# Loading the scale ahead of the shift, and adding the shift to two products afterwards

## The reference

```python
mod = (jax.nn.silu(c) @ w_ada + b_ada).reshape(B, 6, D_MODEL)[:, :, None, :]
sh1, sc1, g1, sh2, sc2, g2 = [mod[:, i] for i in range(6)]
h = rmsnorm(x, norm1_g) * (1 + sc1) + sh1
proj = h @ w_in           # 1024 x 7696: q|k|v, beta, decay, z, pool input, gate_a, gate_b
```

## Time and profile before

| what | value |
|---|---|
| median of 3 runs | 1879.86 us |
| profiled execution | 1879.52 us |
| its span in the trace | 1877.5 us |
| TensorE busy | 1838.3 us, 98% of the span |
| VectorE / ScalarE / GpSimd busy | 82% / 46% / 41% |
| granted TensorE clock, whole span | 0.995 |
| HBM over the span | 252 GB/s |

### The profile page before, as it was taken

The page is one execution under the profiler, slowest core; times in us unless marked ns, Lnnn a source line. Parts: engine busy times, 40 slices in busy tenths (PEclk is TensorE's granted clock), DMA queues, the critical chain, the costliest instruction groups (busy, mean ns, idle before and its releaser), DMA issues.

```text
span 1877.5 us, 34737 instructions
## 1 busy us (share of the span) xinstructions
PE 1838.3 (98%) x13193; PEld 1669.2 (89%) x13193; DVE 1539.7 (82%) x3073; ACT 869.0 (46%) x1535; POOL 769.9 (41%) x572
## 2 busy tenths in 40 slices
PE   6999999999999999999999999999999999999998
PEld 3789999999878999999999888888888889888886
DVE  4667777777666889989794889899899899998998
ACT  3525544545342335688886434333333333333433
POOL 0000000000034435887782445555455555555662
PEclk8999999999999999999999999999999999999999
DMA  9732222222552326686778999999999999999984
GB/s 394 274 129 82 78 85 84 76 86 76 183 200 86 117 94 209 213 237 189 233 204 246 352 373 382 388 387 391 381 375 381 389 389 371 373 381 369 373 336 149
DMA packets 179732, 474.78 MB, mean 253 GB/s; under 512 B 16752, under 2 KB 79184, under 8 KB 176240
## 3 DMA queue, kind: packets, MB, share of 16 engines
q1 hardware_dynamic: 133488, 304.78, 46.5%
q0 software_dynamic: 46080, 167.79, 23.4%
HBM read 426.57 MB, written 45.94 MB: 252 GB/s over the span
## 4 chain that ended last, share of the span: by engine, by line
PE 54%; DVE 11%; DMA 2%; issue 1%; POOL 1%; ACT 0%; DVEq 0%; ACTq 0%
PE dd L2862 17%; PE pp L2849 16%; PE pp L2862 9%; PE pp L2466 7%; PE dd L2817 4%; DMA x<-in_v,idx 1%; POOL hot_a L2628 1%; DVE top_i L2509 1%; DVE top_i L2498 1%; DVE less L2499 1%; DVE top L3107 1%; DVE top_v L2504 1%; DVE top_v L2493 1%; PE pp L469 1%; DVE cand L3219 1%
## 5 line engine op out<-in xcount | busy, mean ns | idle before, releaser
L453 ACT ACTIVATE w_hi<-w_raw 128x1024 fp32r<-128x1024 f32 x202 | 212.8, 1054 | 146.1 <-PE pp L469 88.9
L457 DVE TENSOR_TENSOR w_lo<-w_raw,w_hi 128x1024 fp32r<-128x1024 f32 x176 | 216.2, 1229 | 31.2 <-ACT w_hi L453 31.0
L469 PE MATMUL pp<-act_hi,w_hi 128*128 128x272 f32 x1040 | 233.2, 306 | 1.0 <-POOL w_lo L2483 0.6
L469 PE MATMUL pp<-act_hi,w_lo 128*128 128x272 f32 x1040 | 214.8, 288 | 0.0
L469 PE MATMUL pp<-act_lo,w_hi 128*128 128x272 f32 x1040 | 214.5, 288 | 0.0
L3044 ACT ACTIVATE co_hi<-cf 128x384 fp32r<-128x384 f32 x126 | 66.3, 526 | 318.9 <-PE pp L2862 255.7
L2849 PE MATMUL pp<-act_hi,w_hi 128*128 128x384 f32 x616 | 208.8, 339 | 0.0
L2849 PE MATMUL pp<-act_lo,w_hi 128*128 128x384 f32 x616 | 207.6, 337 | 0.0
L2849 PE MATMUL pp<-act_hi,w_lo 128*128 128x384 f32 x616 | 207.1, 336 | 0.0
L2628 POOL TENSOR_SCALAR hot_a<-cst,gcols 128x128 f32<-128x128 f32 x144 | 190.2, 1329 | 40.4 <-PE dd L2817 40.0
L3337 DVE TENSOR_TENSOR v_lo<-v_raw,v_hi 128x1024 fp32r<-128x1024 f32 x126 | 154.0, 1222 | 28.8 <-ACT v_hi L3032 27.7
(11 more groups left out here) (501 smaller groups left out, 4584.3 us busy)
## 6 DMA issues: line engine op xcount, KB each, us to landing
w_raw<-in_stream SPq DMA_DIRECT2D x206, 512.0 KB
v_raw<-in_v SPq DMA_DIRECT2D x128, 512.0 KB
ada_w<-in_ada SPq DMA_DIRECT2D x24, 1024.0 KB, 10.6
gt<-gate_matrix SPq DMA_DIRECT2D x31, 768.0 KB, 9.2
gate_matrix<-gstage SPq DMA_DIRECT2D x11, 2048.0 KB, 10.3
early<-cst SPq DMA_DIRECT2D x50, 192.0 KB
cst<-early SPq DMA_DIRECT2D x50, 192.0 KB
wrow<-in_wout SPq DMA_DIRECT2D x8, 512.0 KB, 8.2
```

The source lines that it names most:

```text
L453: nc.scalar.activation(w_hi[k.slot][:], w_raw[k.slot][:], ACT.Copy).then_inc(w_hi_done, 1)
L457: nc.vector.tensor_tensor(w_lo[k.slot][:], w_raw[k.slot][:], w_hi[k.slot][:].bitcast(F32), ALU.subtract).then_inc(w_lo_done, 1)
L469: last = nc.tensor.matmul(pp[s][:, b, 0:HN], w[:, c * P:(c + 1) * P], a[:, c, b * HN:(b + 1) * HN], start=(c == 0 and w is w_hi[s] and a i ...
```

## The change

- The 8 MB for shift 1 and scale 1 are laid out anew: four pieces with the scale columns alone, each for two k, then four with the shift columns. The scale pieces are loaded first, chunk 0 ahead of them and chunk 1 behind them; then come the shift pieces.
- `modulate(k, half)` multiplies half a piece: 4 matmuls of 256 columns.
- The squares of x are summed over k by VectorE (7 additions, 128 x 544), so that the matmul with ones runs once instead of 8 times. ScalarE loads one table set for the logarithm and the exponential that follow.
- `h1` is made without the shift: x times scale times reciprocal root in one instruction for each k. Chunks 0 and 1 are multiplied with it. The shift modulates run between (before k = 7 of chunk 0).
- `shift_products(r)`: once the shift is there, 16 matmuls for each of chunks 0 and 1 multiply the weights, still in their buffers, with the 9 shift columns (20 and 10 columns wide with the low part and padding). The result is added when the pooling inputs are copied out (as the bias of `pool_evac`) and, for the samples, in `pool_group`.
- For chunk 2 onward `act_hi` and `act_lo` are made again with the shift in them: `shifted_hi(k)` on ScalarE and `shifted_low(k)` on VectorE, each once chunk 1 has used its k. GpSimd then adds the shift to `h1[k]` (8 instructions of 128 x 512), which only the beta and decay product reads.
- That product moves from behind chunk 1 to behind chunk 3, with pieces 9 and 10 behind it, then its folding and pieces 11 to 13. The cumulative sums of the decay move from in front of chunk 4 to behind it.
- SyncE's list: chunk 2 right behind the shift pieces; piece 8 waits for two shift modulates, with chunk 3, the beta and decay weights and all the rest behind it; pieces 11 to 13 stand behind chunk 4, 14 to 17 behind chunk 5.

```diff
@@ gpsimd
+                for k in range(KC):
+                    pool.wait_ge(h1_hi2, k + 1)
+                    pool.wait_ge(h1_lo2, k + 1)
+                    nc.gpsimd.tensor_scalar(h1[:, k, 0:TP], h1[:, k, 0:TP], mod[:, SH1 + k, 0:1], None,
+                                            ALU.add).then_inc(h1_whole, 1)
@@ sync
-                    if last is not None:
-                        sp.wait_ge(ada_used, last + 1)
+                    sp.wait_ge(ada_used, KC + last + 1 if last >= KC else KC + 2 * last + 2)
...
-                for i in range(KC):
-                    load_ada(i)
                 load_chunk(sp, Chunk(0))
+                for n in range(ADA_BUFS):
+                    sp.dma_start(ada_w[ADA_BUFS + n][:], ada_in[n]).then_inc(ada_ld[ADA_BUFS + n], 16)
                 load_chunk(sp, Chunk(1))
+                for n in range(ADA_BUFS):
+                    sp.dma_start(ada_w[n][:], ada_in[ADA_BUFS + n]).then_inc(ada_ld[n], 16)
+                load_chunk(sp, Chunk(2))
                 load_ada(8)
+                load_chunk(sp, Chunk(3))
...
                 load_chunk(sp, Chunk(4))
+                for i in range(11, 14):
+                    load_ada(i)
                 load_chunk(sp, Chunk(5))
+                for i in range(14, 16):
+                    load_ada(i)
@@ tensor
+                def modulate(k, half):
+
+                    pe.wait_ge(ada_ld[ADA_BUFS * (1 - half) + k // 2], 16)
+                    for j in range(4):
+                        last = nc.tensor.matmul(dd[32 * j:32 * j + NG, ADA_BANK[0], 256 * half:256 * (half + 1)], c_silu[:, k, :],
+                                                (scale_w, shift_w)[half][k][:, 256 * j:256 * (j + 1)],
+                                                start=(k == 0), stop=(k == KC - 1))
+                    last.then_inc(ada_used, 1)
...
+                    pe.wait_ge(shifts_ready, 1)
+                    to = dd[:, 2 + r, 256:256 + 2 * (NG + 1)]
+                    for c in range(KC):
+                        nc.tensor.matmul(to, w_hi[r][:, c * P:(c + 1) * P], shifts[:, c, :, :].rearrange("p s g -> p (s g)"),
+                                         start=(c == 0), stop=False)
+                        last = nc.tensor.matmul(to[:, 0:NG + 1], w_lo[r][:, c * P:(c + 1) * P], shifts[:, c, 0, :],
+                                                start=False, stop=(c == KC - 1))
+                    last.then_inc(pp_done[r], 1)
...
                 for c in range(KC):
-                    first_chunk(c)
-                    if c >= 5:
-                        ada(range(4 + c, 5 + c))
+                    scaled_chunk(0, c)
                     if c >= 3:
-                        second_chunk(c - 3)
+                        scaled_chunk(1, c - 3)
+                    if c == KC - 2:
+                        for k in range(KC):
+                            modulate(k, 1)
+                turn(1)
                 for c in range(KC - 3, KC):
-                    second_chunk(c)
-
+                    scaled_chunk(1, c)
+                for r in range(2):
+                    shift_products(r)
+                ada(range(8, 9))
+                for s in (own_hi, own_lo):
+                    pe.wait_ge(s, 1)
+                for c in range(KC):
+                    last = early_chunk(Chunk(2), c, h1_hi2, h1_lo2)
+                last.then_inc(pp_done[Chunk(2).slot], 1)
+
+                product(pe, Chunk(3))
                 pe.wait_ge(wba_ld, 32)
+                pe.wait_ge(h1_whole, KC)
+                pe.wait_ge(h1_own, 1)
...
-                product(pe, Chunk(2))
+                ada(range(9, 11))
                 pe.wait_ge(ba_out, 2)
...
-                ada(range(12, 14))
-                product(pe, Chunk(3))
+                ada(range(11, 14))
+                product(pe, Chunk(4), range(KC // 2))
                 ada(range(14, 16))
+                product(pe, Chunk(4), range(KC // 2, KC))
...
-                product(pe, Chunk(4), range(KC // 2))
-                turn(1)
-                product(pe, Chunk(4), range(KC // 2, KC))
+                turn(2)
                 ada(range(16, 17))
@@ vector
+                    nc.vector.scalar_tensor_tensor(out=h1[:, k, 0:TP], in0=x[:, k, 0:TP], scalar=aff1[:, k, 0:1],
+                                                   in1=rstd1[:, 0:TP], op0=ALU.mult, op1=ALU.mult).then_inc(h1_done, 1)
...
                 nc.vector.tensor_tensor(tmp_b[:], tok[:, ETOT], tok[:, GCUM], ALU.subtract).then_inc(gc_read, 1)
+                conditioning(2)
                 first_column(1, range(CW))
-                conditioning(1)
```

More of the change, by code:

```diff
@@ L662, in first_chunk, with scaled_chunk @@
                                                     stop=(c == KC - 1 and a is act_lo))
[L663 to L669, removed]
+                    if used is not None:
+                        last.then_inc(used, 1)
+                    return last
+                def scaled_chunk(r, c):
+                    early_chunk(Chunk(r), c, h1_hi_done, h1_lo_done, scaled_used if r else None)
@@ L670, in _ @@
+                for k in range(2):
+                    modulate(k, 0)
+                pe.wait_ge(sq1_summed, 1)
+                for b in range(2):
+                    last = nc.tensor.matmul(pp[0][:, b, 0:HN], ones, sq1[:, 0, b * HN:(b + 1) * HN], start=True, stop=True)
+                last.then_inc(ss1_done, 1)
+                for k in range(2, KC):
+                    modulate(k, 0)
                 turn(0)
-                ada(range(8, 9))
                 pe.wait_ge(rs1_done, 1)
                 for c in range(KC):
-                    first_chunk(c)
-                    if c >= 5:
-                        ada(range(4 + c, 5 + c))
+                    scaled_chunk(0, c)
@@ L733, in _ @@
                 product(pe, Chunk(C_HEADS), range(0, 1))
-                turn(2)
+                turn(3)
                 product(pe, Chunk(C_HEADS), range(1, 2))
@@ L821, in _ @@
                 first_evac(1)
-                ada_evac(1)
+                ada_evac(2)
                 first_square(1)
@@ L900, in _, with shifted_low, bias_summed @@
                 low(KC - 1)
+                def shifted_low(k):
+                    dve.wait_ge(h1_hi2, k + 1)
+                    nc.vector.scalar_tensor_tensor(out=act_lo[:, k, 0:TP], in0=h1[:, k, 0:TP], scalar=mod[:, SH1 + k, 0:1],
+                                                   in1=act_hi[:, k, 0:TP].bitcast(F32), op0=ALU.add,
+                                                   op1=ALU.subtract).then_inc(h1_lo2, 1)
+                def bias_summed(r):
+                    done(dve, Chunk(r))
+                    two = dd[:, 2 + r, 256:256 + 2 * (NG + 1)].rearrange("p (s g) -> p g s", s=2)
+                    nc.vector.tensor_reduce(first_bias[:, r, :], two[:, 0:NG, :], AX_X, ALU.add).then_inc(bias_read, 1)
+                conditioning(1)
+                shift = mod[:, SH1:SH1 + KC, :]
+                st(nc.vector.tensor_copy(shifts[:, :, 0, 0:NG], shift))
+                st.settle()
+                nc.vector.tensor_tensor(shifts[:, :, 1, 0:NG], shift, shifts[:, :, 0, 0:NG].bitcast(F32),
+                                        ALU.subtract).then_inc(shifts_ready, 1)
+                nc.vector.tensor_tensor(sample_cols(h1), sample_cols(h1), b, ALU.add).then_inc(h1_own, 1)
+                for k in range(2):
+                    shifted_low(k)
+                dve.wait_ge(own_hi, 1)
+                nc.vector.tensor_tensor(act_lo[:, :, TP:NT], own, act_hi[:, :, TP:NT].bitcast(F32),
+                                        ALU.subtract).then_inc(own_lo, 1)
+                bias_summed(0)
+                shifted_low(2)
+                split_lo(dve, Chunk(2))
+                shifted_low(3)
+                bias_summed(1)
+                for k in range(4, KC):
+                    shifted_low(k)
+                split_lo(dve, Chunk(3))
                 dve.wait_ge(pool_ld, 16)
@@ L1042, in _ @@
                     pool_read(n)
-                conditioning(2)
+                conditioning(3)
                 affine(aff2, SC2, "g2")
```

137 lines of the change are left out of this document (85 added, 52 removed).

## The result

The changed kernel takes 1887.74 us (median of 6 runs, 1884.99 to 1888.79), the kernel before 1880.85 us (6 runs beside it on the same chip, 1879.79 to 1882.84). The ratio is 1.0035, with an interval of 1.0025 to 1.0046: slower by 6.9 us. The profiled execution took 1887.96 us, its span is 1886.2.

What follows compares the result with a forecast made beforehand. TensorE's gapless list was taken to bound the first block. Start -11.4, list +8.0, gaps +1.0, clock +0.8, pieces +2.0 and decay sums +2.6 gave +3.0 on 1879.5: 1882.5 us, range 1876.5 to 1888 (8 in 10).

Steps and rivals of the forecast that it cites:

- rival 3: First block: more gaps than counted (later clock rise +1.6, third product's cover gone +1, slower shift_products +1.3); 1885 to 1887, chance 0.20.
- (c): Weight pieces 13 and 15 land late because their buffers come free later; TensorE waits 1.0 us for each, 2.0 together.
- the list: Work added to TensorE's list behind the start: shift modulates, piece 8, shift_products, two transposes, less saved switches; +8.0 us.
- rival 2: GpSimd's adds become the bound ahead of the beta and decay product; at 2.5 us each 1885.1 us, chance 0.10.
- rival 4: The early start doesn't come about, layout or queue holding the scale back (29 instead of 26.5); 1885.0 us, chance 0.05.
- Start: TensorE's first product begins at 26.5 instead of 37.98, as four pieces are awaited instead of eight; -11.4 us.
- the case for which I had 25.3: First product starts at 25.3 instead of 26.5 if the clock is full there.
- the term for grouping: Pieces and small work standing in groups save five TensorE switches at about 0.2 us each; -1.1 us.
- (a): At the first k, VectorE's slower h1 and chunk 1's split make TensorE wait near 30 us; 1.0 us.
- (b): Clock at the start: half until 31.7, 4.2 us at half instead of 3.3; +0.8 us (0 to 2.4).
- (d): Decay sums behind chunk 4 delay VectorE's chain; TensorE waits 2.6 us somewhere between norm_sums(1) and pool_out(1).
- The first: Rival: the gaps don't form, 4.6 us less, 1877.9 us; chance 0.22, half of that below 1876.1.

Runs made afterwards that it cites:

- run 3: Changed kernel with pieces 9 and 10 again before chunk 3 and the decay sums again between chunk 4's halves: 1880.91 us, 0.9999 of the kernel before.
- run 8: As run 3, with one of four column blocks in each shift modulate (16 matmuls instead of 64): 1881.13 us, one run.
- run 2: Changed kernel with pieces 9 and 10 multiplied in front of chunk 3 again: 1882.69 us, 1.0010 of the kernel before.
- run 4: Kernel before, with only the beta step, its fold, the decay sums and the pieces and steps belonging to them moved back: 1884.90 us, ratio 1.0024.
- run 11: Changed kernel with a second 128 x 512 GpSimd instruction (times one) behind each of the eight adds: 1899.70 us, one run.
- run 12: Changed kernel with GpSimd's adds on the first 128 of 512 columns only: 1889.54 us, one run.
- run 5: As run 3, with the shift modulates in pairs behind k = 1, 2, 4 and 5 of chunk 0: 1881.70 us, 1.0003 of the kernel before.
- run 6: As run 3, with two shift modulates ahead of the first product and piece 11 ahead of the fold: 1881.71 us, 1.0006 of the kernel before.
- run 10: As run 3, with each row of narrow shift matmuls run twice (64 instead of 32): 1886.98 us, one run.
- run 1: Changed kernel with the decay sums between chunk 4's halves again and first_column(1) ahead of conditioning(2): 1886.14 us, 1.0022 of the kernel before.

## Why the prediction was right or wrong

The direction held (3 us slower forecast, 6.9 measured), though the prediction gave 0.50 to no change that could be told and 0.38 to slower. 1887.74 lies in the range, close to its end; it is outside the likeliest case of 1880.5 to 1884.5. It is in the range by luck more than by the mechanism. The upper end, 1888, stood for rival 3 with its three terms together (1.6 + 1.0 + 1.3 = 3.9 us), and only the first of them came, at 0.3. The 3.9 us that were missing came mostly from elsewhere: (c) 1.6, the clock behind it 1.5, the list 0.8. By the prediction's own sign (wrong if the last matmul ends after 121) it failed, with 122.64. Its other sign, over 1 us more behind the first block, was met too, by the 1.8 us of the two spans. The chances also don't add up as told: rivals 2, 3 and 4 (0.35) and the quarter of the forecast above 1883.6 (0.11) make 0.46 for slower, not 0.38. Point by point:

- *What bounds.* The block ended when TensorE's list ended, and its shift of 6.9 us is the shift of the medians. Right.
- *Start.* 26.5 forecast, 26.43 measured, and the first `h1` at 24.85 for 25.1. But the clock was full there (1.00 in every window from 18 to 28 us), the case for which I had 25.3. The last six scale modulates took 4.14 us, 0.69 for a k, where the shift modulates took 0.46 at the same clock. Why isn't shown, so part of this hit is luck. The reading of TensorE's waits, too, left out the first and longest, 10.9 us until the squares of x are there (L595), which changes nothing here.
- *List.* It came out 0.8 longer than summed, and not by the added work. From the starts in TensorE's timeline, less 0.25 us for each product pair, the shift modulates cost 3.77 (4.0 forecast), the two transposes 0.22 (0.4), the narrow row 3.56 (3.5) and piece 8 1.08 (1.2): 8.6 in all for 9.1. What is left of the 8.8 is 0.2, where the term for grouping had -1.1. So that saving, taken from two rows at other places, did not come. This is by subtraction; no run tested it. The folding was the right neighbour for the narrow matmuls, and the 2.6 us by the Trainium skill's 81 ns a pair ("TensorE: Matmul & The Clock Gate", Back-to-back issue gap) would have been too little: the trace has 0.11 a matmul.
- *(a)* 1.0 for 1.0, but at k = 1 (0.28) and k = 2 (0.71).
- *(b)* The end of the half clock was put at 31.7 and measured at 35.2. The size was wrong as well, the other way: 4.2 us at half instead of 3.3 are 0.9 more, which at 0.45 cost 0.4, not 0.8. The two errors nearly cancel, and 1.1 was measured. Rival 3 had the rise put off by gap (a). That isn't borne out: up to 37 us runs 3 and 8 are the same program, and in both profiles the first product starts at 25.86 and the gap of 0.71 ends at 30.26. Yet the same two matmuls behind it took 0.82 us in run 3, where the clock rose at 34.2, and 0.52 in run 8, where it had risen at 30.2:

```profile
30.26 0.82 PE L678 MATMUL pp<-act_lo,w_hi 128*128 128x272 f32 x2 [0.71 <-DVE act_lo L971]
```

```profile
30.26 0.52 PE L678 MATMUL pp<-act_lo,w_hi 128*128 128x272 f32 x2 [0.71 <-DVE act_lo L971]
```

What sets the rise is open.

- *(c)* The mechanism was right, the size wrong: 1.23 us at piece 13 (1.0 forecast), 2.40 at piece 15 (1.0). From the end of piece 13's matmuls (72.5) TensorE had 3.1 us of product and 1.0 of piece 14 ahead of it, as forecast. The landing was late: piece 13 landed at 71.5 and piece 15 at 79.1, 7.6 us apart, where I had counted 2.5 pieces at 2.49 = 6.2. The window of that stretch, and the issues of pieces 15 and 16 on SyncE:

```profile
71.50:79.10 7.60, 5.22 (x40) 3.28 (x40) 3.01 (x5) 5.99 (x11) 0.75 (x2) 1.00 1.02 428
```

```profile
69.51 0.33 SPq L551 DMA_DIRECT2D ada_w<-in_ada  x1
...
70.37 0.33 SPq L551 DMA_DIRECT2D ada_w<-in_ada  x1
```

DMA was full, and moved 7.6 x 428 GB/s = 3.25 MB, where chunk 5 and pieces 14 and 15 are 2.62 MB. So 0.6 MB of something else went beside them. Piece 16, issued 0.86 us behind piece 15, is the nearest candidate; piece 17 and chunk 6, issued at 72.62 and 72.99, are others. I had let a piece land as if nothing behind it in the queue took a share. No run held any of them back, so this is argued. Shown is that an earlier release of the buffers ends both waits (run 2).

- *What (c) brings with it* is the step that failed most plainly, since it was put at nothing without a reason: half clock behind the wait, 1.5 us. In the earlier trace rows TensorE is at half after it had stood, and I used that for the start alone. Together with (c)'s size it is 3.1 of the 3.9 us that were missing; the list's 0.8 makes the rest.
- *(d)* 2.6 forecast, 2.4 measured, within the stretch named (0.39 at `norm_sums(1)`, 1.75 at `pool_out(1)`), and run 4 shows it without all the rest. A chain with eleven members summed from rows came within 0.2 us.
- *GpSimd.* 1.3 us an add was wrong: 1.9 (1.55 to 2.30), between my bounds of 0.63 and 2.5. It is nearer the 2.2 of rival 2, for which I had no working, than my 1.3. The point of decision stood right: 8 adds began at 46.9 and at 1.9 each ended 1.5 us before TensorE asked; run 11 drove them over it. Rival 2 failed, but by 0.2 us an add, so 0.10 for it was low.
- *Rivals.* The first, that the gaps don't form, is excluded by the waits. The fourth too. The third is nearest: more gaps than counted, though of its three terms only the later rise of the clock came, its reason isn't borne out, and the gaps that were larger were those of (c).

## What to carry to other kernels

Before an earlier start of the bound engine is counted as a gain, its whole list behind that start has to be priced again: what ran under the DMA wait (8.6 us here) becomes work, and the producers and buffers that were on time for a late start are late for an early one. In an order written out by hand, a small step that is moved behind a product takes its whole chain with it (the decay sums: 2.4 us at a pooling step 18 us later, in an otherwise unchanged kernel too), and a buffer ring releases only as early as its last reader stands in that order. A wait of 2 us costs more than 2 us if TensorE's clock falls behind it (3.4 to 6.8 us at half behind the wait for piece 15, some 1.5 to 3 us), so such a wait should be priced with the half clock that the rows show behind others of its kind. It doesn't always come: behind 1.75 us at `pool_out(1)` the clock stayed full in four profiles (the changed kernel, runs 2, 4 and 11) and fell in one (run 12). And two returns at one place have to be undone together before either is judged.

## What the runs showed of the hardware

- **Half clock beside narrow matmuls.** In runs 5, 6, 8 and 10 the granted clock fell to 1.2 GHz during or just behind the row of 128 x 20 and 128 x 10 matmuls, with TensorE shown busy all along, and stayed there 6.8 us. The fall came 2.3 to 5.3 us behind the first of them. In the profiled executions of the changed kernel and of runs 1, 2, 3, 11 and 12 the same row of 32 left the clock full. One thing goes with it: in all six of these the half clock at the start had lasted 6.8 us, and in runs 5, 6 and 8 only 3.4. (Run 10, with twice the row, had 6.8 there too.) No run tested that, and what decides is open. The runs that differ only in this row are 3 and 10, and 10 has one execution; so that the row causes the fall is suggested, not settled. Each such stretch takes some 3 us (6.8 x 0.45). Run 5 had 3.4 us less of half clock at the start (as run 8 had, whose start is that of run 3) and 6.8 more here: 3.4 x 0.45 = 1.5 of the 1.7 us by which its last matmul is behind that of run 3.
- **GpSimd and VectorE slow each other.** A GpSimd add of 128 columns took 0.60 to 1.63 us, one of 512 columns 1.55 to 2.30. VectorE's `shifted_low` took 0.90 us beside the long adds (3.60 for four) and 0.72 beside the short ones (2.88), and a pooling sum 1.14 (3.43 for three) against 0.88. The Trainium skill ("GPSIMD Engine Reference", Key points) says that GpSimd shares its SBUF interfaces with VectorE and contends with VectorE instructions with two SBUF inputs. Both of these are such instructions, and the trace agrees: they took 25% to 30% longer beside the long adds.
- **Four column blocks at once.** 64 modulate matmuls of 9 columns of weights, in four column blocks, take 3.64 us and 16 in one block 3.62.
